# Four pairs of weight tiles moved by multiples of 64 bytes against the tiles they are multiplied with

## The reference, cut to what matters

```python
def peer(h, w_query, sub_keys, u_experts, v_experts):      # per chunk of 128 tokens
    ...
    idx = e1 * PEER_KEYS + e2                # 8 heads x 16 experts of 16384, for each token
    g = jax.nn.softmax(vs, axis=-1)
    u_sel, v_sel = u_experts[idx], v_experts[idx]
    z = jnp.einsum('td,thkd->thk', xc, u_sel)
    a = (jax.nn.gelu(z) * g)
    return jnp.einsum('thk,thkd->td', a, v_sel)
```

## Time and profile before

| | |
|---|---|
| median of 3 runs | 1348.16 us (1343.06, 1348.16, 1351.22) |
| the profiled execution's own time | 1346.72 us |
| its span, first to last instruction | 1345.4 us |
| mean granted TensorE clock | 0.990 of full |
| PE busy | 1280.8 us, 95% of the span |
| PEld busy | 1114.5 us, 83% |
| DVE busy | 1063.8 us, 79% |
| ACT busy | 596.4 us, 44% |
| POOL busy | 252.7 us, 19% |
| read from HBM | 254.47 MB, 190 GB/s over the span |

### The profile page before, as it was taken

One profiled execution on the slowest core, in us unless ns is written; L12 is line 12 of the kernel. 1 busy time (PEld: TensorE's weight loads), 2 busy tenths in 40 slices (PEclk: granted clock), 3 DMA queues, 4 the chain that ended last, 5 costly groups with the idle time before them and its releaser, 6 DMA issues.

```text
span 1345.4 us, 21959 instructions
## 1 busy us (share of the span) xinstructions
PE 1280.8 (95%) x8283; PEld 1114.5 (83%) x8283; DVE 1063.8 (79%) x2318; ACT 596.4 (44%) x1105; POOL 252.7 (19%) x180
## 2 busy tenths in 40 slices
PE   5988999988999899999999999999999999999997
PEld 5577855685697569999999999999988888888886
DVE  5587896787777688999997888888977777777776
ACT  1434683536344535455544444444343333343342
POOL 0363000450000006789950000000000000000001
PEclk9999999999999899999999999999999999999999
DMA  9877631867577245554444444444455555555552
GB/s 356 290 231 271 235 137 60 300 210 264 206 278 273 104 168 178 173 185 158 171 143 156 142 147 152 142 156 141 157 204 191 199 189 196 194 191 196 191 192 106
DMA packets 92382, 256.82 MB, mean 191 GB/s; under 512 B 9472, under 2 KB 16896, under 8 KB 91904
## 3 DMA queue, kind: packets, MB, share of 16 engines
q1 hardware_dynamic: 59728, 195.91, 42.0%
q10 hardware_dynamic: 32560, 59.66, 12.4%
HBM read 254.47 MB, written 1.06 MB: 190 GB/s over the span
## 4 chain that ended last, share of the span: by engine, by line
PE 62%; DVE 13%; POOL 8%; issue 7%; DMA 5%; ACT 3%; SPq 1%; POOLq 0%; ACTq 0%; DVEq 0%
PE bank L1734 25%; PE bank L1727 19%; PE bank L691 5%; PE bank L2006 4%; PE bank L1121 3%; POOL v_lo L1766 2%; POOL u_lo L1766 2%; DVE arena L432 2%; DVE arena L968 2%; PE bank L799 2%; DMA arena<-in_w_in 2%; POOL head_ms L822 2%; DMA arena<-in_nsa_w_in 1%; DVE u_lo L683 1%; ACT arena L976 1%
## 5 line engine op out<-in xcount | busy, mean ns | idle before, releaser
L1727 PE MATMUL bank<-h_hi,u_hi 128*128 128x256 f32 x632 | 182.8, 289 | 3.9 <-POOL u_lo L1766 2.8
L1727 PE MATMUL bank<-h_hi,u_lo 128*128 128x256 f32 x632 | 178.7, 283 | 0.0
L1727 PE MATMUL bank<-h_lo,u_hi 128*128 128x256 f32 x632 | 178.7, 283 | 0.0
L1727 PEld LDWEIGHTS bank<-h_hi,u_hi 128*128 128x128 f32 x632 | 121.0, 191 | 4.7 <-POOL u_lo L1766 1.9
L2163 POOL TENSOR_SCALAR raw<-raw 128x1024 f32<-128x1024 f32 x1 | 3.4, 3356 | 631.7 <-DMA raw<-in_final_g 631.7
L1727 PEld LDWEIGHTS bank<-h_lo,u_hi 128*128 128x128 f32 x632 | 121.1, 192 | 0.0
L1727 PEld LDWEIGHTS bank<-h_hi,u_lo 128*128 128x128 f32 x632 | 120.9, 191 | 0.0
L2102 ACT ACTIVATE u_hi<-raw 128x1024 fp32r<-128x1024 f32 x64 | 67.9, 1061 | 104.4 <-PE bank L1734 104.4
L1727 PE MATMUL bank<-h_hi,v_hi 128*128 128x256 f32 x392 | 112.8, 288 | 0.8 <-POOL v_lo L1766 0.8
L2102 ACT ACTIVATE v_hi<-raw 128x1024 fp32r<-128x1024 f32 x64 | 67.9, 1061 | 101.1 <-PE bank L1734 101.1
L1727 PE MATMUL bank<-h_hi,v_lo 128*128 128x256 f32 x392 | 110.8, 283 | 0.0
(11 more groups left out here) (275 smaller groups left out, 3486.5 us busy)
## 6 DMA issues: line engine op xcount, KB each, us to landing
raw<-in_u SPq DMA_DIRECT2D x128, 512.0 KB, 3.5
raw<-in_v SPq DMA_DIRECT2D x128, 512.0 KB, 4.3
arena<-in_ada_t SPq DMA_DIRECT2D x80, 512.0 KB, 5.2
arena<-in_ada_w SPq DMA_DIRECT2D x12, 512.0 KB, 12.2
raw<-in_nsa_w_in ACTq DMA_DIRECT2D x3, 2048.0 KB, 12.0
arena<-in_moba_w_in ACTq DMA_DIRECT2D x3, 2048.0 KB, 16.5
arena<-in_w_in ACTq DMA_DIRECT2D x3, 2048.0 KB, 10.3
arena<-in_w_query ACTq DMA_DIRECT2D x3, 2048.0 KB, 10.7
```

What stands on the lines that cost most here:

```text
L1727: last = pe.matmul(zbank[k].t[:, 0:S], u[:, c, :], h[:, c, :], start=n == 0, stop=n == 3 * DC - 1)
```

## The change

Only addresses change. The eight halves are no longer allocated ahead of h but behind the tiles of a; ahead of each pair of halves stands a tile of 16 float32 values (64 bytes in each partition) that nothing uses. Instructions, their order on every engine, semaphores and sizes are the same.

```diff
@@ -47,6 +47,7 @@
 RING = 3
 ARENA = 32768
 LINE = 32
+APART = 16
@@ -227,13 +228,16 @@
     gate_row = [sb(f"gate_row{i}", [P, D]) for i in range(2)]
     ones = sb("ones", [P, P])
     hkT = sb("hkT", [P, 3, S])
-    split = {}
-    for name in ("u", "v"):
-        split[name] = [[sb(f"{name}_{part}{k}", [P, D], F32R) for k in range(2)] for part in ("hi", "lo")]
-    quad = [(split[n][0][k][:], split[n][1][k][:]) for n in ("u", "v") for k in range(2)]
     h_hi, h_lo = sb("h_hi", [P, DC, S], F32R), sb("h_lo", [P, DC, S], F32R)
     raw_all = sb("raw", [P, 4, D])
     a_hi, a_lo = ([sb(f"a_{part}{k}", [P, S], F32R) for k in range(2)] for part in ("hi", "lo"))
+    split = {name: [[None, None], [None, None]] for name in ("u", "v")}
+    for name in ("u", "v"):
+        for k in range(2):
+            sb(f"apart_{name}{k}", [P, APART])
+            for part, parts in zip(("hi", "lo"), split[name]):
+                parts[k] = sb(f"{name}_{part}{k}", [P, D], F32R)
+    quad = [(split[n][0][k][:], split[n][1][k][:]) for n in ("u", "v") for k in range(2)]
     cols = sb("cols", [P, NCOL])
```

## The result

The changed kernel takes 1354.29 us in the median of 10 runs (1350.3 to 1355.53), the kernel before 1346.8 (10 runs); the ratio is 1.0051 with a 95% interval of 1.0035 to 1.0066. So it is slower, by 7 us, well outside the noise. The forecast was no change, 1347.5 us; the range (1314 to 1358) holds the time.

What follows compares the result with a forecast made beforehand. The prediction took PE's fp32r matmuls to bound the second and third stages, and POOL's subtractions with PE the first. All terms were zero, so the sum was 0 us and the forecast the runs' mean, 1347.5 us; range 1314 to 1358.

Steps and rivals of the forecast that it cites:

- no change: Whole kernel: the new addresses alter no duration that counts; 0 us, about 1342 to 1354 us with the spread, chance 0.60.
- What bounds the kernel: Expert layer: PE without a gap in the second and third stages, 653 us together; POOL's subtractions and PE in the first.
- The 13 ns above the columns' own time: Each fp32r matmul at full clock: about 13.3 ns that aren't columns, none at half clock; the only large thing addresses could touch.
- the one on the fp32r matmuls: L1727, L1734 and L691: setting the operands 64 to 256 bytes apart changes no matmul's duration; 0 us.
- The evidence of chunks and slots: L1727: pieces over different slots cost 119.6 to 120.1 ns a matmul, so no distance that is a multiple of 512 matters.
- ACT, DVE and POOL: Their work on the slots: covered by PE in the second and third stages; 0 us, 1.3 us either way in the first.
- Rival A: fp32r matmuls: offset starts remove the surplus; 15.8 us at L1734, 16.9 at L1727, 4.4 at L691, 37 in all; chance 0.25.
- Rival B: fp32r matmuls: starts off 128-byte lines cost an extra piece; 10.2 us slower for streamed halves, 32.6 with weight loads; chance 0.15.

Runs made afterwards that it cites:

- the run with h apart: Against the kernel before: halves behind a without pads, 64 unused bytes between h and raw, so raw, a and all slots lie 64 past h; 1343.14 us, ratio 0.9964.
- the run that should have told which load it is: Against the run with h apart: both a_lo tiles moved to 32 bytes before the slots, a_hi at 0; one run, 1351.81 us.

## Why the prediction was wrong, point by point

**What bounds the kernel:** right. PE has no slack in stages 2 and 3, the only thing that moved there is the step, and the time followed it. The 13 ns above the columns' own time were rightly taken for the place that addresses could touch, though the step above the columns then went up to 21 ns at L1734 as well as down to 7 at L1727. They are absent at half clock with the new distances too.

**The step that failed** is the one on the fp32r matmuls: "What the trace can't show is a distance of 64 to 256 bytes. I take zero for it". Its term was 0; measured it is -3.8 us in stage 2 and +6.2 us in stage 3. The first reason, that the two streams pass through all offsets below 512 whatever their start, rested on no row: none shows when a load reads its 512 bytes. The pure distances refute what was concluded from it: 226.9 ns at 0 and 234.5 at 160. The second, that ACT and DVE in the same tiles don't disturb PE, is true in the rows but says nothing of TensorE's two operands against each other. The evidence of chunks and slots was read rightly (multiples of 512 don't matter, and the run with the slots 512 bytes past h agrees), but it covers a single residue, and the argument went on from there to the rest.

**ACT, DVE and POOL:** VectorE's subtraction is at 1226 ns in the third stage as before, so zero was right for their own durations. In stage 1 the term was "1% of 125 us, 1.3 us either way"; 2.5 us were measured. That bound rested on the spread of durations of the subtractions alone. What differs is how long VectorE's other instructions are when POOL is at work, and the first gates wait for these; the prediction had only POOL on this stage's path, although its own window has VectorE busy 119.8 of 125 us against POOL's 113.7.

**Rival A** was right for one half: the start of the two operands against each other decides, and 64 bytes can take part of the surplus. On u's product it gave 8.4 of its 16.9 us in the run with h apart. Where it erred is v's product, of which it expected 15.8 us and which no distance made cheaper than 0 does. The Trainium skill, page "TensorE: Matmul & The Clock Gate", section "Step-by-step: what each phase is for", says that loading the next weights doesn't take read bandwidth from the running matmul. These runs sit badly with that, but don't refute it: for fp32r at full clock a mere displacement of one operand against the other makes the step 113 to 120 ns or 227 to 234 ns long, and no run here shows by which path.

**Rival B** had the right sign, and its low price of 10.2 us for the streamed side is not far from the 6.2 us measured, by luck, for its mechanism is refuted: slots and a both at 64 off the line cost nothing, and on L1734 slots 1 and 2 are the dearest (232.6 and 232.9 ns), slot 0 (229.1) and slot 3 (228.8) less.

**The numbers:** the time lies inside the range of 1314 to 1358 and at the lower edge of rival B's case, which had 0.15. That the range holds it is luck too: it was made for a gain on both products or a loss on both, and what came is the difference of a gain on one and a loss on the other. Too much went to no change (0.60), for an edit that touched the one quantity of which the trace held one sample.

## What to carry to other kernels

Where TensorE streams fp32r operands without a gap, measure the step at a few distances between the stationary and the streamed tile (here modulo 256 bytes) before the layout is frozen; 64 bytes on u's product alone were worth 0.4%, and with the same 64 bytes on v's product too nothing was left of it (ratio 0.9991). Give all buffers of a rotation the same distance, since a change from one buffer to the next had an after-effect of some ten matmuls. And a quantity that takes only one value in a trace isn't known to have no effect: many rows at one residue are one sample of it.

## What the runs showed of the hardware

- An fp32r matmul of 256 columns with its own weight load took 113.3, 117.8 or 120.0 ns from start to start, one of 512 columns 226.7 to 234.5, with the same instructions and nothing but the operands' distance changed. At a granted clock of 0.50 the one of 256 columns took 213 to 214 ns in all 17 kernels.
- 113.3 and 120.0 ns are 272 and 288 cycles of 2.4 GHz, 16 and 32 above the 256 columns; 226.7 are 544, 32 above 512. This would fit a collision between the columns and a weight load whose outcome depends on how the two stand when they start. That is a guess: the run that should have told which load it is didn't.
- At distance 64 (64 or 320 bytes) a block kept one of two paces, 113.3 or 117.8 ns, from its first few matmuls to its end.
- VectorE's four tensor_scalar instructions ahead of the first gates took 5.3 us in the kernel before and 7.4 us in the changed one while POOL was subtracting beside them, and 1.1 us a little later.
- The best version found is h 64 bytes before raw, a and all slots: 1343.14 us, ratio 0.9964 to the kernel before.
- Left open: by which path the distance acts; and why VectorE's instructions meet POOL's worse in some of these kernels, which makes the time up to the first gates 2 to 5 us longer and took back about half of what u's product had gained. That only the distance modulo 256 counts is shown at L1727 by 64 against 320 bytes, and at L1734 by one slot of the changed kernel alone.
